# First level of both triangular inverses on four quadrants, with stacked narrow weights and a reordered RWKV round

## The reference

```python
def rwkv7_time_mix(...):          # per token, per head
    sa = einsum('bhvk,bhk->bhv', state, kk_t)
    state = state * w_t - sa[..., None] * (kk_t * a_t) + v_t[..., None] * k_t

def gated_delta_rule_chunked(q, k, v, g, beta):
    A = where(strict, beta * kk * decay, 0)
    sol = triangular_solve(A + eye, rhs, lower=True, unit_diagonal=True)

z = h @ w_in     # 4096 wide columns and 2 * DN_HEADS = 16 narrow ones (beta, alpha)
```

## Time and profile before

| | |
|---|---|
| Median of 3 runs | 2101.6 us (2101.54 to 2101.67) |
| Span of the profiled execution | 2102.0 us |
| PE busy | 2062.4 us, 98% |
| PEld busy | 1699.5 us, 81% |
| DVE busy | 1131.0 us, 54% |
| ACT busy | 780.5 us, 37% |
| POOL busy | 160.7 us, 8% |
| DMA | 182.65 MB, mean 87 GB/s |
| Mean granted clock | 0.997 of full speed |

### The profile page before, as it was taken

How to read it: one execution, slowest core, us unless ns; L and a number is a source line. 1 busy time by engine, 2 the same in 40 slices (tenths; PEclk the granted TensorE clock), 3 DMA queues, 4 the chain that set the end, 5 groups by cost and what they waited for, 6 DMA issues and landing times.

```text
span 2102.0 us, 33182 instructions
## 1 busy us (share of the span) xinstructions
PE 2062.4 (98%) x13322; PEld 1699.5 (81%) x13322; DVE 1131.0 (54%) x1463; ACT 780.5 (37%) x1182; POOL 160.7 (8%) x118
## 2 busy tenths in 40 slices
PE   8999999999799999999999999999999999999998
PEld 6888888777768888888888888877888888888886
DVE  6444444678767444444444443469777675444322
ACT  5233223483434223322323232246665453233221
POOL 0000011002302000011000001101111120000010
PEclk9999999999999999999999999999999999999999
DMA  5222322320022222322222232221111122222321
GB/s 183 100 93 97 113 96 81 106 78 14 11 74 91 100 99 91 115 97 89 91 94 95 100 109 98 86 80 62 51 51 42 58 86 99 100 90 100 111 97 52
DMA packets 48265, 182.65 MB, mean 87 GB/s; under 512 B 6320, under 2 KB 6576, under 8 KB 48048
## 3 DMA queue, kind: packets, MB, share of 16 engines
q1 hardware_dynamic: 48176, 181.39, 25.1%
HBM read 179.27 MB, written 2.10 MB: 86 GB/s over the span
## 4 chain that ended last, share of the span: by engine, by line
PE 69%; DVE 2%; ACT 1%; issue 0%; POOL 0%; DVEq 0%; ACTq 0%; POOLq 0%
PE banks L614 21%; PE banks L615 21%; PE banks L616 21%; PE banks L1225 1%; PE banks L1194 0%; PE banks L1176 0%; PE banks L1264 0%; PE banks L1047 0%; PE banks L1266 0%; PE banks L1245 0%; PE banks L1242 0%; PE banks L1150 0%; PE banks L1130 0%; PE banks L1006 0%; DVE WS L1989 0%
## 5 line engine op out<-in xcount | busy, mean ns | idle before, releaser
L614 PE MATMUL banks<-H,WS 128*128 128x512 f32 x1840 | 727.6, 395 | 8.4 <-DVE H L2073 8.0
L615 PE MATMUL banks<-H,WS 128*128 128x512 f32 x1840 | 717.0, 390 | 0.0
L616 PE MATMUL banks<-H,WS 128*128 128x512 f32 x1840 | 716.9, 390 | 0.0
L1340 ACT ACTIVATE WS<-RAW 128x1024 fp32r<-128x1024 f32 (+1 forms) x306 | 345.0, 1128 | 909.4 <-PE banks L616 905.5
L1989 DVE TENSOR_TENSOR WS<-RAW,WS 128x1024 fp32r<-128x1024 f32 (+1 forms) x306 | 400.9, 1310 | 193.6 <-ACT WS L1340 193.2
L614 PEld LDWEIGHTS banks<-H,WS 128*128 128x128 f32 x1840 | 345.7, 188 | 85.1 <-DVE WS L1989 9.2
L616 PEld LDWEIGHTS banks<-H,WS 128*128 128x128 f32 x1840 | 345.7, 188 | 72.5
L615 PEld LDWEIGHTS banks<-H,WS 128*128 128x128 f32 x1840 | 345.9, 188 | 70.2 <-issue 1.2
L614 PE MATMUL banks<-A,WS 128*128 128x512 f32 x704 | 273.9, 389 | 0.0
L616 PE MATMUL banks<-A,WS 128*128 128x512 f32 x704 | 273.9, 389 | 0.0
L615 PE MATMUL banks<-A,WS 128*128 128x512 f32 x704 | 273.9, 389 | 0.0
(11 more groups left out here) (406 smaller groups left out, 1657.6 us busy)
## 6 DMA issues: line engine op xcount, KB each, us to landing
RAW<-in_w_gate SPq DMA_DIRECT2D x88, 512.0 KB, 3.2
RAW<-in_w_up SPq DMA_DIRECT2D x88, 512.0 KB, 3.2
RAW<-in_w_down SPq DMA_DIRECT2D x64, 704.0 KB, 4.0
RAW<-in_c_in SPq DMA_DIRECT2D x32, 512.0 KB, 3.2
RAW<-in_ab_in SPq DMA_DIRECT2D x22, 512.0 KB, 3.2
RAW<-in_ab_out SPq DMA_DIRECT2D x8, 512.0 KB, 5.0
RAW<-in_c_out SPq DMA_DIRECT2D x8, 512.0 KB, 3.2
X<-in_x SPq DMA_DIRECT2D x4, 512.0 KB, 7.5
```

Source lines behind the costliest of these rows:

```text
L614: pe.matmul(bank[:, :], high[:, cols], upper, start=first and j == 0, stop=False)
L615: pe.matmul(bank[:, :], high[:, cols], lower, start=False, stop=False)
L616: mm = pe.matmul(bank[:, :], low[:, cols], upper, start=False, stop=last and j == len(rows) - 1)
L1340: act.activation(WS[:, 0, c % SPLIT, 0:cols] if dst is None else dst, RAW[:, c % RING, 0:cols], ACT.Copy).then_inc(hi_ready, 1)
```

## The change

On PE the first level of both inverses walks the crossing order of the later levels. Its transposed operand must then lie crossed for the last four chunks: ACT copies it, two copies of 64x256 for each pair, into the free tile TT (in the DeltaNet into c_TTH), with a new semaphore. In the DeltaNet each result of the first level now lies in two banks and is read by two instructions. The narrow columns' weights are stacked as 32 columns, so two products for each block do, and the sum of the two halves is made in the step that turns to token order, by eight fp32 products with the identity instead of four transposes. In the RWKV rounds the inside products go pair by pair, the wait for the copies moves into the loop behind the first two products, and in the second round turned tokens and first xx of z = 0 come before the key products, as do the first mask and the second first turn on DVE.

```diff
@@ pe_first_u, pe_first_xx @@
-                for r, c in chunk_blocks():
-                    mm = pe.matmul(head_block(4 * z, r, c), w["TM"][r, c, :], w["XX"][r, c, :], start=True, stop=True)
+                for a, f, c in four_ways:
+                    mm = pe.matmul(head_block(4 * z, f, c), w["TM"][a, c, :], w["XX"][a, c, :], start=True, stop=True)
...
-                for r, c in chunk_blocks():
-                    mm = pe.matmul(head_block(4 * z, r, c, upper=True), w["XT"][r, c, :], w["IU"][r, c, :], start=True, stop=True)
+                pe.wait_ge(xt1_crossed[z], 2 * q + 2)
+                for a, f, c in four_ways:
+                    mm = pe.matmul(head_block(4 * z, a, c, upper=True), w["XT" if c < TT else "TT"][f, c, :], w["IU"][f, c, :],
+                                   start=True, stop=True)
@@ PE, RWKV rounds @@
+                            pe_first_xx(q, 0)
                         else:
                             pe_first_u(q, 0)
+                            pe.wait_ge(xx_read[1], 5)
+                            tokens_turned(4, AL, 0, upper=False, across=False)
+                            pe_first_xx(q, 0)
                             key_products(q, 0)
                             key_products(q, 1)
-                            pe.wait_ge(xx_read[1], 5)
-                            tokens_turned(4, AL, 0, upper=False, across=False)
-                        pe_first_xx(q, 0)
...
                         inside_inner(q, 0)
+                        inside_outer(q, 0)
                         inside_inner(q, 1)
-                        inside_outer(q, 0)
                         inside_outer(q, 1)
-                        pe.wait_ge(token_read[0], 2 * q + 2)
                         with pe.Fori(1, 4) as l:
                             pe_level_u(q, 1, l)
                             pe_level_xx(q, 0, l)
+                            pe.wait_ge(token_read[0], 2 * q + 2)
@@ PE, narrow columns @@
-                            for a, b in ((0, 0), (1, 0), (0, 1)):
-                                mm = pe.matmul(BANK[5][0:2 * HEADS, :], CTS[:, b, k, :], H_PARTS[a][:, k, :],
+                            for a in range(2):
+                                mm = pe.matmul(BANK[5][0:4 * HEADS, :], CTS[:, k, :, :].rearrange("p b h -> p (b h)"), H_PARTS[a][:, k, :],
...
-                            tr = pe.transpose(BANK[7][:, j * 16:(j + 1) * 16], TF[0:2 * HEADS, j * P:(j + 1) * P],
+                            for b in range(2):
+                                tr = pe.matmul(BANK[7][:, j * 16:(j + 1) * 16], TF[0:4 * HEADS, j * P:(j + 1) * P],
@@ PE, DeltaNet core @@
-                                for r, e, c in blocks:
-                                    mm = pe.matmul(u_bank[r, c], C_TM[r, e, :], C_XX[r, e, :], start=True, stop=True)
+                                for r, f, e in crossing:
+                                    mm = pe.matmul(first_block(f, e), C_TM[r, e, :], C_XX[r, e, :], start=True, stop=True)
...
+                                pe.wait_ge(*c_xt1_crossed(2 * p + 2))
+                                for r, f, e in crossing:
+                                    mm = pe.matmul(first_block(r, e, upper=True), (C_XT if e < TT else C_TTH)[f, e, :], C_IU[f, e, :],
@@ ACT, RWKV rounds @@
+            def first_crossed(q, z):
+                act.wait_ge(xt1_ready[z], q + 1)
+                for r in (slice(0, CHUNK), slice(CHUNK, P)):
+                    act.activation(INV[z]["TT"][crossed(r), TT:NCHUNK, :], INV[z]["XT"][r, TT:NCHUNK, :], ACT.Copy).then_inc(xt1_crossed[z], 1)
...
+                first_crossed(q, 0)
                 tokens_copied((KT, BT)[q], 0, 4, False, 4 * q + 5)
                 level_copied(q, 0, 0)
+                first_crossed(q, 1)
@@ ACT, DeltaNet core: after the third piece, ahead of the level loop @@
+                        act.wait_ge(*c_xt1(p + 1))
+                        for r in (lo, hi):
+                            act.activation(C_TTH[crossed(r), TT:NCHUNK, :], C_XT[r, TT:NCHUNK, :], ACT.Copy).then_inc(c_xt1_crossed.sem, 1)
@@ DVE, RWKV rounds @@
                         if q:
+                            level_masked(q, 0, 0)
+                            first_turn(q, 1)
                             masked(q, 0, 1)
-                        masked(q, 0, 2)
-                        level_masked(q, 0, 0)
-                        first_turn(q, 1)
+                            masked(q, 0, 2)
+                        else:
+                            masked(q, 0, 2)
+                            level_masked(q, 0, 0)
+                            first_turn(q, 1)
@@ DVE, DeltaNet core @@
-                                vec.tensor_tensor(C_IU[:, :, :], halves(u_bank[:, :]), half("minus2"), ALU.mult).then_inc(c_iu.sem, 1)
+                                for s in range(2):
+                                    ins = vec.tensor_tensor(C_IU[:, TT * s:TT * (s + 1), :], first_bank(s), half("minus2")[:, TT * s:TT * (s + 1), :],
+                                                            ALU.mult)
+                                ins.then_inc(c_iu.sem, 1)
```

More of the change, by code:

```diff
@@ L408, in two_banks, with first_bank @@
             return PS[rows, first:first + 2, HALF_BANK * upper:HALF_BANK * (upper + 1)].rearrange("p b (e c) -> p b e c", c=CHUNK)
+        def first_bank(s, upper=False):
+            return halves(BANK[3 + 3 * s][:, HALF_BANK * upper:HALF_BANK * (upper + 1)])
         def mask_by_head(name):
@@ L479, in hybrid_trunk_kernel @@
             (tr_mm, 12), (tr_read, 12), (mean_mm, 4), (dev_ready, 4), (g_mm, 4), (sp_act, 2), (sp_vec, 2),
-            *((k, n) for ks, n in ((mat_mm, 6), (mat_ready, 8), (xt1_ready, 2), (x1_turned, 2), (token_mm, 2), (token_read, 4),
+            *((k, n) for ks, n in ((mat_mm, 6), (mat_ready, 8), (xt1_ready, 2), (xt1_crossed, 4), (x1_turned, 2), (token_mm, 2), (token_read, 4),
                                    (tm_ready, 2), (u_mm, 10), (iu_ready, 10), (xx_mm, 10), (xx_read, 10), (xt_turned, 8)) for k in ks),
@@ L1045, in tail_products @@
                         for k in range(KB):
-                            for a, b in ((0, 0), (1, 0), (0, 1)):
-                                mm = pe.matmul(BANK[5][0:2 * HEADS, :], CTS[:, b, k, :], H_PARTS[a][:, k, :],
-                                               start=k == 0 and a == b, stop=k == KB - 1 and b == 1)
+                            for a in range(2):
+                                mm = pe.matmul(BANK[5][0:4 * HEADS, :], CTS[:, k, :, :].rearrange("p b h -> p (b h)"), H_PARTS[a][:, k, :],
+                                               start=k == 0 and a == 0, stop=k == KB - 1 and a == 1)
                         mm.then_inc(c_tail_mm.sem, 1)
@@ L1054, in tail_token_major @@
                         for j in range(TT):
-                            tr = pe.transpose(BANK[7][:, j * 16:(j + 1) * 16], TF[0:2 * HEADS, j * P:(j + 1) * P],
-                                              con("ident")[0:2 * HEADS, 0:2 * HEADS])
+                            for b in range(2):
+                                tr = pe.matmul(BANK[7][:, j * 16:(j + 1) * 16], TF[0:4 * HEADS, j * P:(j + 1) * P],
+                                               con("ident")[0:4 * HEADS, 2 * HEADS * b:2 * HEADS * (b + 1)], start=b == 0, stop=b == 1)
                         tr.then_inc(c_tail_mm.sem, 1)
@@ L1107, in _ @@
                     lo, hi = slice(0, CHUNK), slice(CHUNK, P)
-                    blocks = [(r, e, slice(e * CHUNK, (e + 1) * CHUNK)) for e in range(NCHUNK) for r in (lo, hi)]
                     crossing = [(r, crossed(r) if e >= TT else r, e) for k in range(TT) for e in (k, TT + k) for r in (lo, hi)]
@@ L1161, in values_turned, with first_block @@
                                 tr.then_inc(c_vtr_mm.sem, 1)
-                        u_bank, x_bank = banks(0)[1], banks(1)[1]
+                        def first_block(rows, e, upper=False):
+                            at_col = HALF_BANK * upper + e % TT * CHUNK
+                            return banks(e // TT)[1][rows, at_col:at_col + CHUNK]
                         for l in range(5):
@@ L1188, in core @@
                             if l == 0:
-                                for r, e, c in blocks:
-                                    mm = pe.matmul(x_bank[r, c], C_XT[r, e, :], C_IU[r, e, :], start=True, stop=True)
+                                pe.wait_ge(*c_xt1_crossed(2 * p + 2))
+                                for r, f, e in crossing:
+                                    mm = pe.matmul(first_block(r, e, upper=True), (C_XT if e < TT else C_TTH)[f, e, :], C_IU[f, e, :],
+                                                   start=True, stop=True)
                             else:
@@ L1739, in core @@
                             if l == 0:
-                                act.activation(C_XX[:, :, :], halves(x_bank[:, :]), ACT.Copy).then_inc(c_xx.sem, 1)
+                                for s in range(2):
```

(4 more changed lines are left out.)

11 lines of the change are left out of this document (5 added, 6 removed).

## The result

The changed kernel takes 2105.34 us (median of 20 runs, 2102.18 to 2107.35), the kernel before 2102.27 in the same comparison (20 runs, 2101.54 to 2103.99). The ratio is 1.0015, 95% interval 1.0009 to 1.0021: 3.1 us slower where 4.4 faster had been forecast, and above the range's upper end of 2100.4. It is less than the 0.2% at which I drew the border.

The account below looks back on a forecast made before the run. A chain over several engines was taken to bound the RWKV inverse, PE the DeltaNet core. RWKV -5.55, narrow columns -0.46 and DeltaNet +1.64 gave -4.4 from 2101.6, so 2097.2 us, range 2094.8 to 2100.4.

Parts of the forecast that it names:

- RWKV rounds: RWKV inverse: DVE's loop may start earlier, by 2.83 us in round 0 and 2.72 in round 1, together -5.55.
- Narrow columns: Narrow columns: eight fewer records save 1.84 us, the fp32 turn costs 1.38 more than the transposes, net -0.46.
- DeltaNet, waits: DeltaNet core: first xx waits for ACT's crossing copies at p = 0, 1, 2; p = 3 gains 0.92; sum +1.64 us.
- more than one stretch below full clock: Whole kernel: a sign that would show the forecast wrong; no size given.
- a new wait in the RWKV loop: RWKV inverse loop: a sign that would show the forecast wrong; no size given.
- with 0.2 for entering the loop: RWKV round 0: after ACT's copies for z = 1, entering the loop adds 0.2 us, so xx is done at 528.84.
- rival (a): RWKV rounds give only half, as ACT's queue or the loop's entry is late: -2.8, total 2099.9 us; chance 0.13.
- shorter by 2.8 in round 0: RWKV, sign of being right: distance from PE's first L708 to DVE's first turn in the loop shrinks by 2.8 us.
- (b): DeltaNet p = 0: the clock falls once more after PE's idle time, costing 1.7 us: 2098.9; chance 0.12.
- (d): DeltaNet: waits pull the clock down at p = 0, 1 and 2, 5.1 us in all: 2102.3; chance 0.05.
- rival (e): First-level products: starts don't get closer than about 25 ns, losing at most 5.3 us: at most 2102.5; chance 0.02.
- Rival (c): DeltaNet core: crossing copies are free and first xx isn't held, gaining 3.68 us there: 2091.9; chance 0.08.

Follow-up runs that it names:

- RWKV part alone: Kernel before with only the four-quadrant first level, crossing copies and new order of the RWKV rounds: 2100.44 us, ratio 0.9991.
- DeltaNet part alone: Kernel before with only the core's four-quadrant first level, masks in two halves and two crossing copies: 2105.43 us, ratio 1.0017.

## Why the prediction was wrong

Taken against the 2100.4 us that before spans at a mean clock of 0.998:

| Term | forecast | measured | from |
|---|---|---|---|
| RWKV rounds | -5.55 | -2.1 | RWKV part alone, its 7 runs at 0.998: 2098.29 |
| Narrow columns | -0.46 | -0.31 | rows of the changed kernel |
| DeltaNet, waits | +1.64 | +1.5 | DeltaNet part alone, its 4 runs at 0.998 |
| DeltaNet, clock | 0 | about +3 | mean clock of the 20 runs 0.9964, so 1.6 steps of 0.001 at 1.85 |
| Sum | -4.4 | +2.1 | measured as a whole: +3.1 |

Two of the prediction's own signs of being wrong came: more than one stretch below full clock, and a new wait in the RWKV loop.

**The first failed step: "with 0.2 for entering the loop".** It was to be the only cost of issue, and half a microsecond more was my end for it. Measured are 1.09 and 1.38 in the loop's first xx and 0.57 and 0.99 before it, 4.0 in both rounds together. Round 1 shows it whole: 2.37 of them stand there, and of the 2.72 forecast nothing came (29.91 us from turn to turn instead of 29.72). The rows had the sign of it: DVE's and PE's waits told me who came last, and I took the time beneath as free, though PE's fetching lay beneath as well. It was rival (a), "the entry of the loop", which I gave 0.13 and sized at -2.8. Quadrants (-1.1) and order (-0.3) both issue the same instructions in less time, and a supply that does not speed up takes much of it back; with the quadrants alone DVE's mask took more of it than the supply. That it is the supply is shown by the loop written out, by half of the inside products left out, and by the new order alone, which exchanged one wait for the other; how many instructions PE holds ahead was not tried.

**The second failed step: the profiled execution as the base.** Its low stretch at 519.65 is rare in the kernel before: its mean clock is 0.997, like that of one run in the 67 of the three batches, and its span of 2102.0 is 1.6 above the usual 2100.4. The forecast's first steps took place inside this stretch ("at half clock it issues in 0.97"), and what was saved there isn't there to save in the other executions. So the sign "shorter by 2.8 in round 0" came true by luck: of 14.84 - 12.08 = 2.76, the unchanged code at full clock (12.86) accounts for 2.0. Of the 3.4 us missing in the table's first row this stretch is about 2, which leaves about 1.4 for the supply. "That execution lies 0.4 above the median" compared a span with a time; the time of a run is about 1.8 more than its span (2107.1 and 2105.3 for the profiled run of the changed kernel), so it lay some 2 above.

**The third: clock, rivals (b) and (d).** They had 0.12 and 0.05. (d) put the falls at p = 0, 1 and 2, 1.7 each; the profiles show p = 0 and p = 2, at 1.55 each in the core's length (233.8 us against 230.7 for the DeltaNet part alone, which has the waits without a fall). "Against: what surrounds that is dense 128x512 work" was no reason: with dense work ahead of the wait the clock fell all the same, and the dense work behind it is what ran at half speed. The mechanism of (d) decided; its total of 2102.3 was too low only because it stood on an RWKV gain of 5.5.

**What was right.** First-level products of 0.69, and so no spacing of 25 ns between starts: the 32 records of 0.69 are about 15 ns apart, against the rule of the Trainium skill (TensorE: Matmul & The Clock Gate, "Wait — 56ns, not 53.3ns?"), as the row of before had said; rival (e) falls. (Beside that rule the prediction wrote 0.80 us for 32 records. With the 0.22 of the last record it is 1.0, as rival (e) reckons it.) The three waits for c_TTH with their sizes, none at p = 3, the SC step held by POOL at p = 0 (1.02 us against 0.16 in the kernel before, where it ended before POOL began), the wait for YI gone, the crossing copies of the RWKV hidden. Rival (c) is right as a mechanism: with the copies ahead of the tap nothing waits for them. It is wrong in size, since DVE's masks then pace the core.

What stays open: why the clock fell at p = 0 and p = 2 in both profiles of the changed kernel and not in that of the DeltaNet part alone, with the same waits; the one with half of the inside products left out fell for p = 2 alone. The 1.85 for a step of the mean clock comes from one kernel's 11 runs; the changed kernel's 20 give 1.6 and 1.75 for the first two steps, and nothing more for its one run at 0.995. And 1.0 us of the sum: by the parts the changed kernel at 0.998 should span 0.9 less than before, while its 2 runs there (mean 2101.0) span 0.6 more. Each part's interval reaches 1.9 us to either side, so this isn't settled. The profiles offer a place for it: the RWKV stage takes 58.5 us in the RWKV part alone, and 59.9 and 59.3 in the two profiles of the changed kernel, which wait 0.6 and 0.8 longer in the same products for "issue" and have the same code there.

## What to carry to other kernels

When a wait of the matmul engine is to be removed in code with many short instructions, first ask whether its instructions come faster than it issues them: list the fetch packets of the stretch beside the waits, and count a wait as gained only as far as the packets' spacing allows. A loop, whose turns fetched nothing here, gives PE time to catch up; written out it cost 10.9 us. When copies are added for a faster product, place them in the queue by when their input is ready and not after work that waits for someone else: here two copies of 0.85 us in all, behind a tap, turned a gain into a loss. Where PE works without a gap, a new wait like these (1.8 and 2.8 us) is to be priced with a stretch at half clock behind it (1.5 to 1.9 us here), and the mean clock of each run tells roughly how often that comes.

## What was not expected of the hardware

- PE's instructions arrive in packets of 16 KB that were never less than 3.3 us apart in these stretches, whatever waited for them; a group of 32 matmuls and 32 weight loads of 64x64 issues in about 0.5 us (L732 at 527.32, L742 at 527.79), so a chain of such groups outruns them.
- With equal waits (6.3 and 6.4 us in three) one execution keeps full clock and another falls twice.
- A DVE step on SBUF alone that starts 0.2 to 0.3 us after a POOL tensor operation was held: 1.02 us for 128x8 against 0.35 behind the mask and 0.16 with POOL idle, 1.42 against 0.75 for 128x512. The one step that began just before POOL's (0.06) was not.
